# Two transformer blocks in float32 on one core: the boundaries between layers are reordered

## The chip, the cores and the metric

The kernel runs on one core of one Trainium2 chip. A core has TensorE (PE, matmuls into the eight banks of PSUM), VectorE (DVE), ScalarE (ACT), GpSimd (POOL, hardly used here) and SyncE (SP), whose queue issues all the DMAs of this kernel. Each engine runs its own instructions in order and waits on semaphores for the others. The metric is the device time of one launch in microseconds (us).

## The reference, cut to what is computed

Batch 1, 256 rows, width 2048, everything float32. The first block is a transformer block with a modulation from a vector c; the second has attention with compressed, selected and windowed keys, a pooling branch, cross attention to a memory, and a second feed-forward layer.

```python
ada = silu(c) @ w_ada + b_ada                 # shift, scale, gate for mixer and FFN
h = rms_norm(x, g_pre_mix) * (1 + scale_m) + shift_m
z = h @ w_in ; o = concat(mla(z), gla(z)) @ w_out
x = x + gate_m * rms_norm(o, g_post_mix)
h = rms_norm(x, g_pre_ffn) * (1 + scale_f) + shift_f
x = x + gate_f * rms_norm((silu(h @ w_ffn_gate) * (h @ w_ffn_up)) @ w_ffn_down, g_post_ffn)
# second block
z = rms_norm(x, ln_mix_pre) @ w_in_2          # 2048 x 7728
y = (g_a * (nsa(z) @ w_br_attn) + g_p * (pool(z) @ w_br_pool)) @ w_mix_out
x = x + rms_norm(y, ln_mix_post)
x = x + rms_norm(cross(rms_norm(x, ln_x_pre) @ w_xq, mem) @ w_xo, ln_x_post)
h = rms_norm(x, ln_ffn_pre)
x = x + rms_norm((silu(h @ w_gate) * (h @ w_up)) @ w_down, ln_ffn_post)
```

## The kernel before

**Tiling.** The 256 rows are two row blocks r = 0, 1 of 128 partitions (`RB`), and the width is 16 tiles of 128 (`KT`). The running sum is `X`. A product needs its left operand transposed: a *turn* takes 8 groups of two width tiles. For a group b PE transposes four 128x128 pieces into one bank (L1016), ACT rounds it to `XTh`, and DVE writes the rest, value less rounded value, to `XTl`. Turns used banks 4 and 5 in alternation (`PB[4 + g % 2]`), so PE could be two groups ahead of DVE (`turn_free`).

**Slabs.** Weights come in slabs of 1 MB (four width tiles by 512 columns, 454 in the first half of `w_in_2`), in a ring of four buffers `raw`. ACT rounds a slab to `wh` (`hi()`, L555), DVE writes the rest to `wl` (`lo()`, L1633), both with two buffers, and PE runs 24 matmuls (`slab_mm`, L1045 to L1047: four tiles, three products, first row block 0, then row block 1). `hi()` of a slab waits until the slab two before it is used up (`slab_used`). SP issues a new slab when DVE has finished with its buffer. Four slabs make a chunk of 512 columns, and a chunk has two banks, one for each row block.

**A layer's end.** The last product of a layer (`wout`, the FFN's `down`, `mix`, `xo`) leaves `ROWB`; ACT (L624) or DVE copies or adds a chunk, ACT squares it with a row sum (`post_square`, L548), DVE weighs it with the gain `G` (`weigh`, L1633). In `add_normed` DVE sums the squares (L1746), ACT takes the root, DVE inverts it (L1678), and eight instructions add the chunks to `X` (L1754); `x_added` counts them.

**A layer's start.** Five turns with their products follow: `f1` (first FFN), `z2` (`w_in_2`), `xq`, `f2`, and `o`, `y` without a norm. For `z2`, `xq` and `f2` the norm is taken after the product: PE turns `X` itself as soon as its chunks are added. For `f1` the norm comes first: ACT squares X in two instructions of 2048 columns (`norm_stats`), DVE inverts, ACT scales row block 0 and DVE row block 1 into `ROWB`, then PE turns `ROWB`; DVE applies scale and shift (`gained`, L1691) before ACT rounds. `turn_into` (L1020) turns four groups, runs slab 0, turns two groups, runs slab 1, and so on; `z2` alone turned all eight groups first (L1369).

**The order** is written out by hand, one stream for each engine. Chunk counts and semaphores are plain numbers.

```python
L1372                for c in range(2):
L1373                    chunk(c, ALL, Z2_PARTS[0][1], free=...)
```

## Time and profile before

| | us |
|---|---|
| median of 3 runs | 2922.84 |
| lowest, highest | 2920.22, 2924.76 |
| the profiled execution | 2926.01 |
| its span, first to last instruction | 2924.2 |
| PE busy (mean granted clock) | 2685.9 (0.954 of full) |
| DVE, ACT busy | 1663.4, 1157.8 |

A timeline row gives start, duration, engine, line and form; xN is a merged run of N instructions, and the brackets name the idle time just before and what ended it. PE's matmuls are pipelined: a row's 0.39 us is longer than its distance from the next.

### The profile page before, as it was taken

How to read it: one execution, taken by the hardware profiler on the slowest of the kernel's cores; microseconds unless marked ns; L12 is line 12 of the kernel's file. 1: busy time of each engine (PE TensorE's matmuls, PEld its weight loads, DVE VectorE, ACT ScalarE, POOL GpSimd, SP SyncE). 2: the span in 40 equal slices, each digit the busy share in tenths (PEclk: the TensorE clock that was granted, in tenths of full speed). 3: DMA queues.
4: the chain of work that ended last, by engine and by line, in shares of the span. 5: the costliest groups of instructions: out<-in, count | busy, mean ns of one | idle time of the engine just before them, and what ended most of it. 6: DMA issues, size and time to landing. Idle time of an engine off the chain costs nothing.

```text
span 2924.2 us, 31137 instructions
## 1 busy us (share of the span) xinstructions
PE 2685.9 (92%) x12176; PEld 2194.6 (75%) x12176; DVE 1663.4 (57%) x1601; ACT 1157.8 (40%) x1200; POOL 0.2 (0%) x4
## 2 busy tenths in 40 slices
...
DMA packets 253356, 565.93 MB, mean 194 GB/s; under 512 B 9647, under 2 KB 52557, under 8 KB 240094
## 3 DMA queue, kind: packets, MB, share of 16 engines
...
## 4 chain that ended last, share of the span: by engine, by line
PE 78%; DVE 8%; ACT 5%; DMA 4%; issue 4%; SPq 1%; DVEq 0%; ACTq 0%
PE bank L1045 23%; PE bank L1047 23%; PE bank L1046 23%; ACT wh L555 3%; DVE wl L1633 2%; DVE ACC L1654 2%; DMA raw<-in_w_ada 2%; DVE ROWB L1633 1%; DMA raw<-in_w_out 1%; DMA raw<-in_w_xkv 1%; PE bank L1016 1%; PE bank L1451 1%; DVE X L1754 1%; PE bank L1503 1%; PE bank L1082 1%
## 5 line engine op out<-in xcount | busy, mean ns | idle before, releaser
L1633 DVE TENSOR_TENSOR wl<-raw,wh 128x2048 fp32r<-128x2048 f32 (+2 forms) x430 | 975.3, 2269 | 912.2 <-ACT wh L555 911.5
L555 ACT ACTIVATE wh<-raw 128x2048 fp32r<-128x2048 f32 (+2 forms) x430 | 816.0, 1898 | 1260.6 <-PE bank L1047 1158.8
L1045 PE MATMUL bank<-wh,XTh 128*128 128x512 f32 (+2 forms) x2712 | 1077.6, 397 | 46.3 <-DVE wl L1633 36.7
L1046 PE MATMUL bank<-wl,XTh 128*128 128x512 f32 (+2 forms) x2712 | 1064.1, 392 | 0.0
L1047 PE MATMUL bank<-wh,XTl 128*128 128x512 f32 (+2 forms) x2712 | 1063.5, 392 | 0.0
L1045 PEld LDWEIGHTS bank<-wh,XTh 128*128 128x128 f32 x2712 | 520.4, 192 | 158.4 <-DVE wl L1633 31.5
L1047 PEld LDWEIGHTS bank<-wh,XTl 128*128 128x128 f32 x2712 | 518.9, 191 | 103.4
L1046 PEld LDWEIGHTS bank<-wl,XTh 128*128 128x128 f32 x2712 | 520.9, 192 | 99.0
L1045 PE MATMUL bank<-wh,HTh 128*128 128x512 f32 x704 | 276.7, 393 | 9.4 <-DVE HTl L1633 3.6
L1047 PE MATMUL bank<-wh,HTl 128*128 128x512 f32 x704 | 274.2, 389 | 0.0
L1046 PE MATMUL bank<-wl,HTh 128*128 128x512 f32 x704 | 274.1, 389 | 0.0
L1045 PEld LDWEIGHTS bank<-wh,HTh 128*128 128x128 f32 x704 | 132.1, 188 | 46.5 <-issue 14.4
L1047 PEld LDWEIGHTS bank<-wh,HTl 128*128 128x128 f32 x704 | 132.2, 188 | 27.7
L1046 PEld LDWEIGHTS bank<-wl,HTh 128*128 128x128 f32 x704 | 132.2, 188 | 26.6
L1654 DVE SCALAR_TENSOR_TENSOR ACC<-raw,cT,ACC 128x2048 f32<-128x2048 f32 x60 | 141.0, 2350 | 7.2 <-DMA raw<-in_w_ada 2.2
L1633 DVE TENSOR_TENSOR ROWB<-ROWB,bank 128x512 f32<-128x512 f32 x176 | 112.6, 681 | 10.9 <-PE bank L1047 9.0
L1650 DVE SCALAR_TENSOR_TENSOR ACC<-raw,cT,ACC 128x2048 f32<-128x2048 f32 x32 | 75.2, 2351 | 4.2 <-DVE wl L1633 1.6
L1016 PE MATMUL bank<-CON,ROWB 128*128 128x128 f32 x96 | 19.1, 355 | 48.2 <-ACT ROWB L548 17.1
L821 ACT ACTIVATE HTh<-bank 128x512 fp32r<-128x512 f32 x44 | 23.9, 595 | 90.4 <-PE bank L1331 90.4
L1016 PEld LDWEIGHTS bank<-CON,ROWB 128*128 128x128 f32 x96 | 14.2, 180 | 53.3 <-ACT ROWB L548 18.0
L548 ACT ACTIVATE XTh<-bank,vT 128x256 fp32r<-128x256 f32 x70 | 28.8, 471 | 47.7 <-PE bank L1016 47.6
L1016 PE MATMUL bank<-CON,X 128*128 128x128 f32 x96 | 19.8, 375 | 27.3 <-DVE X L1754 17.2
...
## 6 DMA issues: line engine op xcount, KB each, us to landing
...
```

Source lines behind the costliest of these rows:

```text
L555: act.activation(wh[:, st.lin % 2, 0:width], raw[:, st.raw % 4, 0:width], ACT.Copy).then_inc(hi_made, 1)
L1016: mm = pe.transpose(PB[4 + g % 2][:, SEQ * k + P * r:SEQ * k + P * r + P], src(r, 2 * b + k), ident)
L1045: pe.matmul(out_, hi_t[:, k, rows], w[0][:, q, :], start=first and q == 0, stop=False)
L1046: pe.matmul(out_, hi_t[:, k, rows], w[1][:, q, :], start=False, stop=False)
L1047: mm = pe.matmul(out_, lo_t[:, k, rows], w[0][:, q, :], start=False, stop=last and q == n - 1)
L1082: mm = pe.matmul(PB[7][:, k:k + 1], ACC[:, P * k:P * k + P], ones[:, 0:1], start=True, stop=True)
L1451: pe.matmul(PB[2 + u % 2][:, 0:2 * nk].rearrange("p (b n) -> p b n", b=2), QT(i, par, r), KT2(g, nk), start=True, stop=True).then_inc(S("n ...
L1503: pe.matmul(PB[7][:, HD * b:HD * b + HD], pT[:, u % 2, P * blk_:P * blk_ + P], Z2[:, k, c0:c0 + HD], start=k == 0, stop=k == r)
L1633: return dve.tensor_tensor(out_, a, b, op)
L1650: ins = dve.scalar_tensor_tensor(ACC[:, :], w, cT[:, bass.ds(k0 + k, 1)], ACC[:, :], ALU.mult, ALU.add)
L1654: ins = dve.scalar_tensor_tensor(ACC[:, :], w, cT[:, k:k + 1], ACC[:, :], ALU.mult, ALU.add)
L1754: dve.scalar_tensor_tensor(x, y, nstat[:, j, 2, r:r + 1], x, ALU.mult, ALU.add).then_inc(S("x_added"), 1)
```

## The change

- **First row block signalled alone.** The last slab of `wout`, `mix`, `xo` and of both `down` products increments a semaphore (`o_row`, `mix_row`, `xo_row`, `y_row`) after its first 12 matmuls. ACT copies and squares row block 0 then, and row block 1 after `slab_used`; DVE's last `add` does the same. ACT's order becomes copy, square, copy, square.
- **Root table early.** A one-column `Sqrt` into a new tile `warm` stands before the last chunk's copies and squares, so that the table load stands there and no longer behind them.
- **Residual squares per chunk.** For `f1` ACT squares `X` in eight pieces of 512, each when that piece has been added (`fsq`); DVE sums them. Both row blocks are then scaled in pieces of 512, and PE waits for a piece (`f_rows0`, `f_rows1`), not for the row. `mod_fin(4)` moves behind `add_normed("o")`.
- **Turns over four banks.** `f1`, `z2`, `f2`, `y`, `xq`, `o` use banks 4 to 7.
- **Projection begun on two groups.** `z2` is turned as the others are, by `turn_into`, with three `hi()` and three `lo()` in the turn; its loop of 2 x 2 chunks is written out as four chunks, and ACT's norm statistics come after the third `hi()`.

```diff
+WIDE = {"f1", "z2", "f2", "y", "xq", "o"}
+def turn_bank(name, b):
+    return 4 + (b % 4 if name in WIDE else (TURN0[name] + b) % 2)
...
+            def root_ready():
+                act.activation(warm[:, :], eps[:, 0:1], ACT.Sqrt)
+
+            def added_stats(name, ready):
+                j = NORMS.index(name)
+                for c in range(4):
+                    for r in range(RB):
+                        act.wait_ge(S("x_added"), added(ready, c, r + 1))
+                        if 2 * c + r >= 4:
+                            act.wait_ge(S("f_sq"), 2 * c + r - 3)
+                        k = 512 * ((2 * c + r) % 4)
+                        f(JUNK[:, k:k + 512], X[:, r, 512 * c:512 * c + 512], ACT.Square, "f_sq", accum_out=fsq[:, r, c:c + 1])
+                act.wait_ge(S("squared"), RB * j + RB)
+                f(nstat[:, j, 1, :], nstat[:, j, 0, :], ACT.Sqrt, "rooted", scale=1.0 / D, bias=eps[:, 0:1])
...
             def chunk_squared(name, layer, c, done):
+                if c == 3:
+                    root_ready()
+                    n = CHUNK0[layer] + c
+                    for r in range(RB):
+                        act.wait_ge(S(f"{name}_row"), 1) if r == 0 else act.wait_ge(slab_used, done)
+                        act.activation(ROWB[:, r, 512 * c:512 * c + 512], PB[2 * (n % 2) + r][:, :], ACT.Copy).then_inc(chunk_out, 1)
+                        post_square(name, c, lambda r: act.wait_ge(chunk_out, RB * n + r + 1), (r,))
+                    return
...
                 if k == 0:
-                    norm_stats(pre, lambda r: X[:, r, :], D, after)
-                    norm_rows(pre, lambda r: X[:, r, :], lambda r: ROWB[:, r, :])
+                    added_stats(pre, after)
+                    act.wait_ge(S("rooted_inv"), NORMS.index(pre) + 1)
+                    for c in range(4):
+                        f(ROWB[:, 0, 512 * c:512 * c + 512], X[:, 0, 512 * c:512 * c + 512], ACT.Copy, "f_rows0",
+                          scale=nstat[:, NORMS.index(pre), 2, 0:1])
...
-            turn_hi("z2", XTh, gain=vT[:, V_LN_MIX:V_LN_MIX + KT])
+            turn_hi("z2", XTh, gain=vT[:, V_LN_MIX:V_LN_MIX + KT], between=lambda: hi(4 * width))
             norm_stats("z2", lambda r: X[:, r, :], D, "y1")
...
                     g = TURN0[name] + b
-                    if g >= 2:
+                    if name in WIDE:
+                        pe.wait_ge(S("turn_free"), TURN0[name] + max(0, b - 3))
+                    elif g >= 2:
                         pe.wait_ge(S("turn_free"), g - 1)
                     if after:
                         pe.wait_ge(S("x_added"), added(after, b // 2))
+                    if each:
+                        each(b)
...
                     if half and r == 0:
-                        mm.then_inc(S("first_row"), 1)
+                        mm.then_inc(S(half), 1)
...
-            turn("z2", lambda r, k: X[:, r, P * k:P * k + P], lambda: None, after="y1")
-            turned_ready("z2")
-            with pe.Fori(0, 2) as i, st.loop(i, 2, 8, 8):
-                for c in range(2):
-                    chunk(c, ALL, Z2_PARTS[0][1], free=i * 4 + RB * (CHUNK0["zin2"] + c - 1))
+            for c in range(4):
+                chunk(c, ALL, Z2_PARTS[0][1], free=RB * (CHUNK0["zin2"] + c - 1), turning=None if c else (
+                    "z2", lambda r, k: X[:, r, P * k:P * k + P], lambda: None, "y1"))
...
-            mod_fin(4)
             add_normed("o")
+            mod_fin(4)
...
                 if k == 0:
-                    norm_row2(pre)
+                    j = NORMS.index(pre)
+                    dve.wait_ge(S("f_sq"), 4 * RB)
+                    dve.tensor_reduce(nstat[:, j, 0, :], fsq[:, :, :], AX.X, ALU.add).then_inc(S("squared"), RB)
+                    norm_inv(pre)
+                    dve.wait_ge(S("rooted_inv"), j + 1)
+                    for c in range(4):
+                        dve.tensor_scalar(ROWB[:, 1, 512 * c:512 * c + 512], X[:, 1, 512 * c:512 * c + 512],
+                                          nstat[:, j, 2, 1:2], None, ALU.mult).then_inc(S("f_rows1"), 1)
...
-                    add(n, FN - 1, last)
+                    add(n, FN - 1, last, k + 1 if n == 3 else None)
```

ACT between the last product of `w_out` and the turn `f1`, before (psq holds the layer's squares, nstat the norms' sums and roots):

```order
L624 ACTIVATE ROWB<-bank 128x512 x2
L548 ACTIVATE JUNK,psq<-ROWB 128x512 x2
L548 ACT_TABLE_LOAD
L548 ACTIVATE nstat<-nstat,eps 128x2
L548 ACTIVATE JUNK,nstat<-X 128x2048 x2
L548 ACTIVATE nstat<-nstat,eps 128x2
L548 ACTIVATE ROWB<-X,nstat 128x2048
L548 ACTIVATE XTh<-TMP 128x512 x4
```

The same place after the change:

```order
L599 ACT_TABLE_LOAD
L599 ACTIVATE warm<-eps 128x1
L806 ACTIVATE ROWB<-bank 128x512
L556 ACTIVATE JUNK,psq<-ROWB 128x512
L806 ACTIVATE ROWB<-bank 128x512
L556 ACTIVATE JUNK,psq<-ROWB 128x512
L556 ACTIVATE nstat<-nstat,eps 128x2
L556 ACTIVATE JUNK,fsq<-X 128x512 x8
L556 ACTIVATE nstat<-nstat,eps 128x2
L556 ACTIVATE ROWB<-X,nstat 128x512 x4
L556 ACTIVATE XTh<-TMP 128x512 x4
```

The table load stands ahead of the copies, each copy is followed by its square, and the two squares of `X` have become eight.

DVE at the same place, before:

```order
L1633 TENSOR_TENSOR mtmp<-bank,bT 128x16
L1668 SCALAR_TENSOR_TENSOR modA<-mtmp,vT 128x16
L1746 TENSOR_REDUCE nstat<-psq 128x2
L1633 TENSOR_TENSOR ROWB<-ROWB,G 128x512 x2
L1678 RECIPROCAL nstat<-nstat 128x2
L1754 SCALAR_TENSOR_TENSOR X<-ROWB,nstat,X 128x512 x8
L1678 RECIPROCAL nstat<-nstat 128x2
L1732 TENSOR_SCALAR ROWB<-X,nstat 128x2048
L1691 TENSOR_SCALAR TMP<-bank,modA 128x256 x4
L1633 TENSOR_TENSOR XTl<-TMP,XTh 128x512
```

And after:

```order
L1793 TENSOR_REDUCE nstat<-psq 128x2
L1678 TENSOR_TENSOR ROWB<-ROWB,G 128x512 x2
L1723 RECIPROCAL nstat<-nstat 128x2
L1801 SCALAR_TENSOR_TENSOR X<-ROWB,nstat,X 128x512 x8
L1678 TENSOR_TENSOR mtmp<-bank,bT 128x16
L1713 SCALAR_TENSOR_TENSOR modA<-mtmp,vT 128x16
L2012 TENSOR_REDUCE nstat<-fsq 128x2
L1723 RECIPROCAL nstat<-nstat 128x2
L2016 TENSOR_SCALAR ROWB<-X,nstat 128x512 x4
L1738 TENSOR_SCALAR TMP<-bank,modA 128x256 x4
L1678 TENSOR_TENSOR XTl<-TMP,XTh 128x512
```

The two small instructions on `mtmp` and `modA` now stand behind the eight additions to `X`, and a second sum of squares, of `fsq`, has come in.

ACT between the last squares of the first FFN and the first copy-out of `w_in_2`, before (the first rows only of its loop):

```order
L548 ACT_TABLE_LOAD
L548 ACTIVATE nstat<-nstat,eps 128x2
L548 ACTIVATE XTh<-bank,vT 128x256 x16
L548 ACTIVATE JUNK,nstat<-X 128x2048 x2
L548 ACTIVATE nstat<-nstat,eps 128x2
L555 ACTIVATE wh<-raw 128x1816
L857 UNCONDITIONAL_BRANCH
L857 ISA
L554 ISA
L555 ACTIVATE wh<-raw 128x1816
```

And after:

```order
L556 ACTIVATE JUNK,psq<-ROWB 128x512 x2
L556 ACTIVATE nstat<-nstat,eps 128x2
L556 ACTIVATE XTh<-bank,vT 128x256 x8
L563 ACTIVATE wh<-raw 128x1816
L556 ACTIVATE XTh<-bank,vT 128x256 x4
L563 ACTIVATE wh<-raw 128x1816
L556 ACTIVATE XTh<-bank,vT 128x256 x4
L563 ACTIVATE wh<-raw 128x1816
L556 ACTIVATE JUNK,nstat<-X 128x2048 x2
L556 ACTIVATE nstat<-nstat,eps 128x2
L563 ACTIVATE wh<-raw 128x1816 x2
L899 ACTIVATE Z_78<-bank,nstat 128x454 x2
```

The 16 roundings of the turn `z2` are broken into 8, 4 and 4 with one slab's `hi()` behind each, and the norm's squares have moved behind the third of them. On PE the 32 transposes that stood in one row become 16, 8 and 8 with the 24 matmuls of a slab between.

## Rows read from the trace of the kernel before

**Rows 1.** Timeline (start, duration), ACT: end of `wout` to turn `f1`.

```profile
605.26 1.08 ACT L624 ACTIVATE ROWB<-bank 128x512 f32<-128x512 f32 x2 [2.83 <-PE bank L1047]
...
619.98 2.00 ACT L548 ACTIVATE ROWB<-X,nstat 128x2048 f32<-128x2048 f32 x1 [0.30 <-DVE nstat L1678]
```

**Rows 2.** Timeline, DVE: the same place.

```profile
608.73 0.17 DVE L1633 TENSOR_TENSOR mtmp<-bank,bT 128x16 f32<-128x16 f32 x1 [3.67 <-PE bank L1082]
...
609.10 1.28 DVE L1633 TENSOR_TENSOR ROWB<-ROWB,G 128x512 f32<-128x512 f32 x2
...
610.50 5.39 DVE L1754 SCALAR_TENSOR_TENSOR X<-ROWB,nstat,X 128x512 f32<-128x512 f32 x8
...
623.21 1.90 DVE L1691 TENSOR_SCALAR TMP<-bank,modA 128x256 f32<-128x256 f32 x4 [1.94 <-PE bank L1016]
625.03 0.68 DVE L1633 TENSOR_TENSOR XTl<-TMP,XTh 128x512 fp32r<-128x512 f32 x1
```

**Rows 3.** Timeline, PE: turn `f1`, slabs 0 and 1.

```profile
622.09 1.94 PE L1016 MATMUL bank<-CON,ROWB 128*128 128x128 f32 x8 [13.40 <-issue]
...
629.34 0.78 PE L1045 MATMUL bank<-wh,XTh 128*128 128x512 f32 x1
...
636.70 0.60 PE L1016 MATMUL bank<-CON,ROWB 128*128 128x128 f32 x4
...
641.28 0.76 PE L1045 MATMUL bank<-wh,XTh 128*128 128x512 f32 x1 [1.63 <-DVE wl L1633]
```

**Rows 4.** Timeline, DVE, then PE: first FFN's end, turn `z2`, its slab 0.

```profile
1397.15 2.29 DVE L1633 TENSOR_TENSOR wl<-raw,wh 128x2048 fp32r<-128x2048 f32 x1 [1.41 <-ACT wh L555]
...
1408.56 1.66 DVE L1708 SCALAR_TENSOR_TENSOR XTl<-bank,vT,XTh 128x256 fp32r<-128x256 f32 x4
...
1419.49 0.74 PE L1045 MATMUL bank<-wh,XTh 128*128 128x454 f32 x1 [2.12 <-DVE XTl L1708]
```

**Rows 5.** Timeline, ACT: norm squares, `hi()` of slabs 2 and 5 of `z2`.

```profile
1418.14 1.91 ACT L548 ACTIVATE JUNK<-X 128x2048 f32<-128x2048 f32 x1
...
1427.31 1.72 ACT L555 ACTIVATE wh<-raw 128x1816 fp32r<-128x1816 f32 x1 [2.79 <-PE bank L1047]
...
1442.14 1.73 ACT L555 ACTIVATE wh<-raw 128x1816 fp32r<-128x1816 f32 x1 [3.22 <-PE bank L1047]
```

**Rows 6.** Timeline, DVE, then PE: end of `mix`, turn `xq`.

```profile
2075.78 0.16 DVE L1746 TENSOR_REDUCE nstat<-psq 128x2 f32<-128x8 f32 x1 [3.54 <-ACT JUNK L548]
...
2077.52 5.39 DVE L1754 SCALAR_TENSOR_TENSOR X<-ROWB,nstat,X 128x512 f32<-128x512 f32 x8
...
2085.38 0.78 PE L1045 MATMUL bank<-wh,XTh 128*128 128x512 f32 x1
```

**Rows 7.** Timeline, ACT: end of `xo`.

```profile
2149.92 0.63 ACT L548 ACTIVATE JUNK<-ROWB 128x512 f32<-128x512 f32 x1
...
2151.91 1.08 ACT L624 ACTIVATE ROWB<-bank 128x512 f32<-128x512 f32 x2 [1.27 <-PE bank L1047]
...
2154.23 1.28 ACT L548 ACT_TABLE_LOAD   x1
2155.53 0.29 ACT L548 ACTIVATE nstat<-nstat,eps 128x2 f32<-128x2 f32 x1
```

**Rows 8.** Timeline, PE: third and fourth groups of turns `o` and `y`.

```profile
508.90 1.25 PE L1016 MATMUL bank<-CON,Z 128*128 128x128 f32 x8 [1.78 <-DVE XTl L1633]
...
1982.02 1.97 PE L1016 MATMUL bank<-CON,Z 128*128 128x128 f32 x8 [0.56 <-DVE XTl L1633]
```

**Rows 9.** Timeline, DVE: the last `add`, at the kernel's end.

```profile
2911.58 1.29 DVE L1633 TENSOR_TENSOR ROWB<-ROWB,bank 128x512 f32<-128x512 f32 x2 [3.43 <-PE bank L1047]
```

**Rows 10.** Windows: length, busy of PE, PEld, DVE, ACT, POOL; granted clock; DMA share, GB/s.

```profile
1423.00:1426.00 3.00, 3.00 (x11) 2.65 (x11) 1.46 (x1) 1.51 (x1) 0.00 (x0) 0.65 0.00 0
2086.00:2089.00 3.00, 3.00 (x12) 2.41 (x11) 2.07 (x5) 2.40 (x3) 0.00 (x0) 0.78 0.99 384
644.00:648.00 4.00, 4.00 (x13) 3.18 (x12) 0.00 (x0) 0.51 (x1) 0.00 (x0) 0.64 0.41 159
```

More of the change, by code:

```diff
@@ L242, in build @@
         psq = sb("psq", [P, len(POST), RB, 4])
+        fsq = sb("fsq", [P, RB, 4])
+        warm = sb("warm", [P, 1])
         eps = sb("eps", [P, 1])
@@ L1003, in _, with turn @@
             st = Slabs()
-            def turn(name, src, ready, groups=None, after=None):
+            def turn(name, src, ready, groups=None, after=None, each=None):
                 ready()
@@ L1026, in turn_into, with slab_mm @@
                     if s < 2:
-                        turn(name, src, lambda: None, range(4 + 2 * s, 6 + 2 * s), after)
+                        turn(name, src, lambda: None, range(4 + 2 * s, 6 + 2 * s), after, each)
             def turned_ready(name):
                 pe.wait_ge(S("turn_free"), TURN0[name] + TURN_N[name])
-            def slab_mm(banks, kts, width, first, last, lhs=None, half=False, row_free=None):
+            def slab_mm(banks, kts, width, first, last, lhs=None, half=None, row_free=None):
                 hi_t, lo_t = lhs or (XTh, XTl)
@@ L1579, in _ @@
             for c in range(4):
-                chunk(CHUNK0["mix"] + c, ALL, 512, turning=None if c else (
+                chunk(CHUNK0["mix"] + c, ALL, 512, row="mix_row" if c == 3 else None, turning=None if c else (
                     "y", lambda r, k: Z2[:, r, P * k:P * k + P], lambda: pe.wait_ge(S("merged"), 3 * RB * 4)))
@@ L1622, in _ @@
             for c in range(4):
-                chunk(CHUNK0["xo"] + c, [12, 13, 14, 15], 512)
+                chunk(CHUNK0["xo"] + c, [12, 13, 14, 15], 512, row="xo_row" if c == 3 else None)
             ffn(1, "f2")
@@ L2001, in add @@
                     for r in range(RB):
+                        if row is not None and r:
+                            dve.wait_ge(slab_used, used)
                         y = ROWB[:, r, 512 * n:512 * n + 512]
```

75 lines of the change are left out of this document (41 added, 34 removed).

## The prediction

> **What bounds the kernel now.** I read the busy table first: PE works 2685.9 us of a span of 2924.2, DVE 1663.4 and ACT 1157.8. Then the timeline around each layer boundary, one engine at a time, to see which engine's last row releases the next. Inside a layer PE runs slab behind slab and the others wait for it, so nothing saved there on ACT or DVE counts. At a boundary the reverse holds: PE has nothing until the sum `X` is complete and turned. After `wout`, DVE's additions begin at 610.50 and take 5.39 [rows 2], the next transposes start at 622.09 after 13.40 us without a matmul, and slab 0 starts at 629.34 [rows 3]. The change touches only such stretches. What counts is therefore how much closer the first slabs of a layer come to the last matmul of the layer before. All sums are differences within the profiled execution (2926.01, span 2924.2); I subtract them from the median 2922.84, since the profiled one lies 0.1% above it and the stretches are fixed lengths.
>
> **wout to f1: 8.0 us, in three terms.**
> First the tail. Before, ACT starts its two copies at 605.26 [rows 1] and DVE's additions start at 610.50. The sum of squares is held back by `mod_fin`, which DVE does ahead of it and which waits for PE until 608.73; the weighing then takes 1.28 [rows 2]. After, the first row block is signalled half a slab (about 2.7) earlier, near 602.5, inside ACT's idle 2.83 [rows 1]. The table load (1.28) [rows 7] stands there too, so row block 0 is copied and squared (0.54 + 0.63) by 605.3. Row block 1 follows at 605.26: copy, then square with its accumulator read, done by 606.7. DVE reduces at 606.75, and from a reduction to the additions it needs 0.15 + 1.28 + 0.16, here 1.5 with overlaps: additions from 608.27, a gain of 2.2. `mod_fin` now runs behind the additions. Its two instructions of 0.17 [rows 2] end at 614.0, while ACT still squares (below): cost nothing; uncovered it would be 0.35.
> Second the norm. Before, the additions end at 615.89 and the transposes start at 622.09 [rows 2, 3]: 6.2, of which two squares of 2048 columns (1.91 each, row of the same form in [rows 5]) and the scaling of row block 0, 2.00 [rows 1]. After, ACT squares each piece of 512 in 0.63 [rows 7], below the addition's pace of 5.39/8 = 0.67, so it ends one piece behind: additions end at 613.66, squares at 614.42, reduction 0.15, root 0.29, reciprocal 0.17. Scaling starts at 615.25 and PE after its first piece at 615.95, i.e. 2.3 behind the additions instead of 6.2: gain 3.9. ACT's later pieces (0.63 each) stay ahead of PE, which needs 0.97 for a group. DVE's pieces have no row; bounds are 0.4 (row of 256 columns, 1.90/4 less 0.07) and 0.68 [rows 2], and with either they keep pace too.
> Third the turn. Before, with two banks, transposes to slab 0 took 7.25 (622.09 to 629.34) [rows 3]. After, four groups lie in four banks at once, and DVE sets the pace: one group transposed (about 1.1), four `gained` groups less the last (3 x 0.95) and two rests (0.68 each, overlapping a little), 5.4. Gain 1.85. Slab 0 takes until 636.70 and slab 1 starts 4.6 later [rows 3], because DVE does two groups and `lo()` between; that order is unchanged, so this gap stays.
> Sum 2.2 + 3.9 + 1.85 = 8.0.
>
> **y1 and z2: 7.0 us.** At the end of the first FFN the early signal helps nothing: DVE runs its last `lo()` from 1397.15 to 1399.44 [rows 4] and goes from there into the final add, the sum and the additions without a pause. Tail 0. Call T = 1408.56 the end of the additions. Before, eight groups are turned, then slab 0 starts at 1419.49 (T + 10.9) [rows 4]. Slab 2 is being rounded from 1427.31 and slab 5 from 1442.14, each released by the end of the slab two before [rows 5]; so slab 0 ends at 1427.3, slab 3 ends and slab 4 starts at 1442.1 (T + 33.5), and the pitch is 14.83/3 = 4.94 per slab. After, PE has four groups in four banks as the chunks are added, DVE finishes groups 0 and 1 with four rests (1.66) [rows 4] and slab 0 starts at T + 1.7. Slab 0 some 6.4, transposes 1.0, slab 1 4.94: T + 14.1. But the norm is later now: behind slab 1 ACT and DVE still have roundings of the last groups (1.6), a `hi()` (1.72), two squares (3.9), root and reciprocal (0.6), another `hi()` (1.72) and a `lo()` (2.05, the row of 2.29 scaled to 454 columns), 12.1 in all, where PE has slabs 2 and 3 to work on (9.9 and two transposes 1.0). PE runs dry by about 1.2 and slab 4 starts at T + 26.4: 7.0 earlier. The bounds: the 9.2 gained at slab 0 is kept but for the two groups of transposes that now lie behind it (8.5), or the three `hi()` and `lo()` in the turn each hold a slab by 1.5 (4.0). The loop becoming straight code adds no row I can see; its branch instructions lie on idle sequencers.
>
> **The four-bank turns of xq, f2, o and y: 2.7 us.** At `xq` the additions end at 2077.52 + 5.39 = 2082.91 and slab 0 starts at 2085.38 [rows 6], 2.47 later; with groups 2 and 3 already transposed only the four rests of 1.66 remain: 0.8. `f2` is built alike: 0.8. At `o` and `y` PE waited 1.78 and 0.56 for a bank [rows 8]; that wait goes, but `o` is fed by weights that arrive slowly, so I take 0.6 and 0.5. Bounds 0 and 2.3 for the two together.
>
> **Tails of mix, xo and y2: 1.27 - 0.25 + 0.64.** At `mix` the sum of squares comes at 2075.78 [rows 6], after two copies and two squares; with row block 0 done earlier one copy (0.5) and square are left out: 2074.78. The table load (1.28 between squares and root, as in [rows 7]) held the root; without it the additions follow 1.47 behind (0.15 + 1.28 + 0.16 less overlap, as at `wout`): 2076.25 against 2077.52. At `xo` ACT is not idle: it squares chunk 2 until 2150.6 and copies again from 2151.91, with an idle of 1.27 [rows 7]. Load and `warm` (1.5) overrun that idle, and four serial instructions follow; I find the additions at 2156.3 against 2156.06, a loss of 0.25. Bounds: gain 1.3 as at `mix`, loss 1.6. At the kernel's end the two adds take 1.29 together [rows 9]; one of them moves ahead: 0.64.
> The trace has the root 0.02 behind the load's end (2154.23 + 1.28 to 2155.53) [rows 7]. The Trainium skill (ScalarE: Activation LUTs, "What ACT_TABLE_LOAD costs") puts a drain of 1380 ns on top of the load; no pause of that kind stands in this row, and with it `xo` would lose about 1.6 and the total would be 1.4 us smaller. I go by the row.
>
> **Sum.** 8.0 + 7.0 + 2.7 + 1.27 - 0.25 + 0.64 = 19.4. 2922.84 - 19.4 = **2903.5**. SP's queue loses and gains no DMA; a buffer is reissued when DVE's `lo()` is done, which only comes earlier. PE's new waits (`turn_free`, `x_added`, `f_rows`) hold transposes alone, and behind them only the slab that needs them.
>
> **The clock** is the term I can't sum. In windows right after slab 0's start the granted clock is 0.65 at `z2`, 0.78 at `xq`, 0.64 within slab 1 of `f1` [rows 10]: part at 1.2 and part at 2.4 GHz. Slab 0 took 7.4 at `f1` (629.34 to 636.70), 7.8 at `z2` (1419.49 to 1427.31), against 4.94. Where the transposes ran straight into the slab (`xq`) the clock was back sooner than where PE had waited in between. After the change PE transposes four groups in one go, then pauses about 1.4. I take the two as balancing.
>
> **Rivals.**
> A. *The turn warms the clock.* Four groups without a pause count as work, and slab 0 runs at the full clock at `f1`, `z2`, `xq`, `f2`: about 1.8 each (the 2.4 to 2.9 that the rows show at `f1` and `z2`, the 1.1 of `xq`, averaged), 7.2 in all: 2896.3. For: `xq`'s early return. Against: the pause that follows. 0.12.
> B. *The clock comes later.* The new pause, and fewer transposes close to slab 0, leave slab 0 slow at `xq` and `f2` (1.0 each) and slab 1 partly slow at `z2`, `xq`, `f2` as it is at `f1` (2.9 each): 10.7 lost, 2914.2. For: [rows 10] at `f1`. 0.13. Beside it stands the Trainium skill (TensorE: Matmul & The Clock Gate, "Part 4: PE-mode transpose"): transposes don't count as PE-busy in the same way. This trace speaks partly against that, as `xq` shows.
> C. *The waits were covered by something else* (weights at the boundaries arrive no sooner, or the stretch gained is given back at the first slab that waits for DMA): 2922, no change. Against: the ring of four slabs is full through each tail. 0.04.
> D. *Slower.* The turns now split PE's start into short bursts with pauses, and the clock stays at 1.2 GHz through the first slabs. A slab at that level costs another 4.9 (twice the pitch). Four such slabs beyond those of today eat the 19.4, from there it is slower; with 14 (three more at most boundaries) 2922.8 - 19.4 + 69 = 2972. Against: before, slabs behind pauses of 13 us still regained the clock within one or two. 0.03.
> The forecast itself: 0.68, with a range of its own of 2898 to 2909 (`z2` 4 to 8.5, the turns, `xo`).
>
> **Numbers.** 0.2% is 5.8 us, about what a measurement here can tell from no change. Forecast, A and B are all faster by more: 0.93; same 0.04; slower 0.03. The range reaches into A and B: 2895 to 2914.5.
>
> **What the profile after would show.** Additions at `wout` start 3.0 behind ACT's last copy instead of 5.2; the first transposes of `f1` 2.3 behind their end, slab 0 5.4 later, slab 1 still 4.6 behind slab 0's end. At `z2` slab 0 at T + 1.7 and slab 4 at T + 26.4 with a small DVE wait before it. Additions at `mix` 2.9 behind the last matmul's release, at `xo` no earlier. Table loads ahead of the last copies. The forecast is wrong if slab 0 comes on time but the granted clock of the first two slabs differs from today's, if scaling of `ROWB` on DVE falls behind PE, or if `z2`'s norm holds slab 4 by more than 1.2.

## The result, and the profile after

The median of 4 runs is 2905.89 us (2903.01 to 2909.67) against 2923.11 for the kernel before; the ratio is 0.9943, 95% interval 0.9931 to 0.9955: 17 us less, with the interval reaching from 13 to 20. The forecast was 2903.5, its range 2895 to 2914.5. The profiled execution took 2907.55 us, its span is 2905.8, 18.4 shorter than the span before.

The page of the changed kernel, first its busy row, then its chain:

```profile
PE 2678.1 (92%) x12176; PEld 2189.3 (75%) x12176; DVE 1662.8 (57%) x1605; ACT 1160.4 (40%) x1220; POOL 0.2 (0%) x4
...
PE 77%; DVE 9%; ACT 5%; DMA 5%; issue 3%; SPq 1%; DVEq 0%; ACTq 0%
```

PE's work is the same, so what went away is time between its slabs. To say where, I line up the starts of all slabs in the two timelines of PE. "Pause" below is the time from the start of a slab's last matmul to the start of the next slab's first one (0.23 in a gapless row of slabs), "length" that from a slab's first matmul to its 24th (5.21 at full clock for 512 columns, 4.74 for 454). Slab 62 is slab 0 of `f1` in this count, 194 that of `z2`, 276 of `y`, 292 of `xq`, 296 of `xo`, 300 of `f2`.

End of `wout` to `f1` in the changed kernel, timeline of ACT, DVE and PE (start, duration; to be held against [rows 1 to 3]):

```profile
601.19 1.92 ACT L563 ACTIVATE wh<-raw 128x2048 fp32r<-128x2048 f32 x1 [4.29 <-DMA raw<-in_w_ffn_gate]
603.12 1.28 ACT L599 ACT_TABLE_LOAD   x1
604.42 0.20 ACT L599 ACTIVATE warm<-eps 128x1 f32<-128x1 f32 x1
604.52 0.58 ACT L806 ACTIVATE ROWB<-bank 128x512 f32<-128x512 f32 x1
...
605.77 0.58 ACT L806 ACTIVATE ROWB<-bank 128x512 f32<-128x512 f32 x1
```

```profile
607.21 0.16 DVE L1793 TENSOR_REDUCE nstat<-psq 128x2 f32<-128x8 f32 x1 [1.78 <-ACT JUNK L556]
...
608.68 5.39 DVE L1801 SCALAR_TENSOR_TENSOR X<-ROWB,nstat,X 128x512 f32<-128x512 f32 x8
613.99 0.17 DVE L1678 TENSOR_TENSOR mtmp<-bank,bT 128x16 f32<-128x16 f32 x1
...
614.97 0.16 DVE L2012 TENSOR_REDUCE nstat<-fsq 128x2 f32<-128x8 f32 x1 [0.60 <-ACT JUNK L556]
...
615.69 1.67 DVE L2016 TENSOR_SCALAR ROWB<-X,nstat 128x512 f32<-128x512 f32 x4
```

```profile
616.67 3.65 PE L1056 MATMUL bank<-CON,ROWB 128*128 128x128 f32 x16 [7.92 <-DVE ROWB L2016]
622.05 0.79 PE L1085 MATMUL bank<-wh,XTh 128*128 128x512 f32 x1 [1.74 <-DVE XTl L1678]
...
633.94 0.76 PE L1085 MATMUL bank<-wh,XTh 128*128 128x512 f32 x1 [3.55 <-DVE wl L1678]
```

The additions start at 608.68 instead of 610.50, the transposes 2.6 behind their end instead of 6.2, and slab 0 5.4 behind the first transposes instead of 7.25. Slab 1 still starts 4.8 behind slab 0's last matmul.

`z2`, timeline of DVE and of PE (against [rows 4]):

```profile
1392.10 5.39 DVE L1801 SCALAR_TENSOR_TENSOR X<-ROWB,nstat,X 128x512 f32<-128x512 f32 x8
1397.41 3.22 DVE L1755 SCALAR_TENSOR_TENSOR XTl<-bank,vT,XTh 128x256 fp32r<-128x256 f32 x8
```

```profile
1399.11 0.47 PE L1085 MATMUL bank<-wh,XTh 128*128 128x454 f32 x1 [1.81 <-DVE XTl L1755]
...
1423.89 0.44 PE L1085 MATMUL bank<-wh,XTh 128*128 128x454 f32 x1 [1.09 <-DVE wl L1678]
```

With T = 1397.49, the end of the additions, slab 0 starts at T + 1.6 and slab 4 at T + 26.4, after the small wait of 1.1 for `lo()`, behind the norm's squares.

By place, in us gained, from the two profiles. The last two rows hold what no term of the forecast named. All cells together, with `o` at 0, make 18.6, and the span is 18.4 shorter; 2.8 of that (+2.6, -1.1, +1.3) stands at places that the experiments below show to be chance:

| place | forecast | measured | clock beside it |
|---|---|---|---|
| `o` turn | 0.6 | 0.4 in the pause before slab 0, 0 by the end of `wout` | |
| `wout` to `f1` slab 0 | 8.0 | 7.3 | 0 |
| `y1`, `z2` to slab 4 | 7.0 | 6.9, 1.0 of it clock in slab 0 | |
| wait for weights, slab 210 | 0 | -1.4 | -1.4 |
| `y` turn | 0.5 | 0.77 | -0.5 |
| `mix` tail, `xq` turn | 1.27 + 0.8 | 1.21 + 0.85 | -0.7 |
| `xo` tail, `f2` turn | -0.25 + 0.8 | -0.5 + 0.83 | +1.6 (slab 296), +0.9 (slab 300) |
| end | 0.64 | 0.6 | |
| slabs 70, 304, products before slab 118 | 0 | | +2.6, -1.1, +1.3 |
| slab 211 to the end of the second block's attention | 0 | -0.7 | |

### The profile page after: what moved, and what is told of

Read it like the earlier page. It is cut to its first block, busy times and chain, and to the rows that moved or that the text cites. A ratio compares the mean times of both kernels' runs of the same rounds, so it can differ in the third digit from the quotient of the medians.

```text
span 2905.8 us, 31119 instructions
## 1 busy us (share of the span) xinstructions
PE 2678.1 (92%) x12176; PEld 2189.3 (75%) x12176; DVE 1662.8 (57%) x1605; ACT 1160.4 (40%) x1220; POOL 0.2 (0%) x4
## 4 chain that ended last, share of the span: by engine, by line
PE 77%; DVE 9%; ACT 5%; DMA 5%; issue 3%; SPq 1%; DVEq 0%; ACTq 0%
PE bank L1085 23%; PE bank L1087 23%; PE bank L1086 23%; ACT wh L563 3%; DVE wl L1678 2%; DMA raw<-in_w_ada 2%; DVE ACC L1699 2%; DVE ROWB L1678 2%; DMA raw<-in_w_out 1%; DMA raw<-in_w_xkv 1%; PE bank L1496 1%; DVE X L1801 1%; PE bank L1056 1%; PE bank L1548 1%; ACT JUNK L556 1%
## 5 line engine op out<-in xcount | busy, mean ns | idle before, releaser
L1755 DVE SCALAR_TENSOR_TENSOR XTl<-bank,vT,XTh 128x256 fp32r<-128x256 f32 x70 | 29.0, 477 | 24.3 <-ACT XTh L556 24.3
```

## Experiments

Twelve kernels ran in three groups, two of them (the kernel before again, and the one with the loops of `z2`) for their trace only, one run each; the kernel before ran beside each group (medians 2923.04, 2927.31, 2924.06), and ratios are against that.

**The changed kernel and the kernel before, again.** No edit.

> The changed kernel, unaltered, a second time. Theory 1: where the granted clock falls and returns is not fixed by the program, so single slabs differ between two profiles of the same kernel. The slab behind the 3.97 us pause in the first FFN (start 684.59 in the first profile, 5.34 us long there, 8.21 in the kernel before) takes either about 5.3 or about 8.2, the starts of slabs elsewhere shift by the same amounts, and the sum of such differences is 1 to 4 us. Waits that the order of instructions sets (17.2 us before slab 0 of f1, 11.5 before slab 0 of z2, 1.45 before slab 4 of z2) repeat within 0.1. Theory 2: the clock's places are fixed by the program: every slab repeats within 0.1. Time 2903 to 2910 either way. The wait of 3.28 us for a weight slab after the loads of w1 and REL (1.88 in the kernel before): repeats within 0.3 if the change made it, between 1.5 and 3.5 if it is the DMA's own scatter.

Measured: 2904.01 us, ratio 0.9937 (0.9915 to 0.9959). Windows over six slabs that stand behind a pause (slabs 70, 194, 292, 296, 300, 304), one row each: length, busy times, granted clock, DMA share, GB/s. First before, then the changed kernel, then the changed kernel again:

```profile
691.90:700.10 8.20, 8.16 (x23) 6.47 (x24) 5.24 (x4) 1.42 (x1) 0.00 (x0) 0.62 0.52 158
...
2128.20:2135.20 7.00, 7.00 (x24) 5.64 (x25) 2.29 (x1) 0.91 (x1) 0.00 (x0) 0.76 0.36 112
...
2191.90:2199.00 7.10, 7.10 (x24) 5.67 (x25) 2.11 (x1) 1.59 (x3) 0.00 (x0) 0.76 0.85 290
```

```profile
684.60:692.80 8.20, 8.09 (x34) 6.40 (x35) 5.68 (x5) 3.29 (x2) 0.00 (x0) 1.00 0.51 158
...
2112.10:2119.10 7.00, 7.00 (x31) 5.78 (x32) 2.29 (x1) 2.06 (x2) 0.00 (x0) 1.00 0.36 109
...
2173.00:2180.10 7.10, 7.10 (x19) 5.62 (x20) 2.10 (x1) 1.58 (x3) 0.00 (x0) 0.59 0.84 292
```

```profile
679.50:687.70 8.20, 8.18 (x23) 6.51 (x24) 5.22 (x4) 1.39 (x1) 0.00 (x0) 0.62 0.52 161
...
2110.60:2117.60 7.00, 6.97 (x31) 5.75 (x32) 2.29 (x1) 2.06 (x2) 0.00 (x0) 1.00 0.37 104
...
2171.50:2178.60 7.10, 7.07 (x31) 5.87 (x32) 2.17 (x1) 2.89 (x4) 0.00 (x0) 1.00 0.81 286
```

Slab 70 ran at 0.62 before, at 1.00 in the first profile of the changed kernel and at 0.62 in the second: the 2.6 us that the first comparison credits there are chance, and so are the 1.1 at slab 304 and the 1.3 before slab 118 (a pause of 13.06 or 11.7 in profiles of either kernel). Slab 296 is not: 0.76 before, 1.00 in both. The pauses set by the order repeat within 0.05 at `z2` (11.49 and 11.50), `xq` (10.37, 10.36) and `f2` (12.09 twice), but at `f1` the pause is 17.17 and 17.96 us: in the second profile the gate weights landed later, ACT's `hi()` ended at 599.6 and the table load ran behind it, until both copies were late.

> The kernel before, unaltered, a second time, for its trace. Theory: what the order of instructions sets repeats within 0.1 us (24.5 us before slab 0 of f1, 20.75 before slab 0 of z2, 12.4 before xq and f2); slabs behind a pause change between about 5.3 and about 8.2 from profile to profile. Open: the wait for a weight slab behind the loads of w1, 1.88 here and 3.28, 3.28, 3.25, 3.27 and 3.13 in the five profiles of the changed kernel and its variants, and the first slab of xo, 6.97 here and 5.35 to 5.37 in the other five. If both repeat, the change moved them (a transfer and a clock that stand in another place to the pauses before them); if the wait comes out near 3.2 or the slab near 5.4, it was chance.

Measured: 2921.41 us in one run. Slab 70: 5.35 long here, 8.21 in the first profile. Slab 296: 6.93, against 6.97. Slabs 292 and 300: 6.29 both, against 6.22. The wait behind the loads of `w1`: 1.66, against 1.88. So the clock has two kinds of places. At slab 70 and slab 304, and in slabs 0 to 2 of `f1`, it differs from profile to profile (slab 70: 5.35, 6.95 and 8.2 all occur among the fourteen profiles). At `xq` and `xo` it goes with the program: `xo`'s first slab is 6.93 to 6.97 in both profiles of before and 5.34 to 5.39 in all twelve others; `xq`'s is 6.2 to 6.3 and 6.86 to 7.00. Which part of the change moved them stays open, since no run that takes one part back restores them. `y` and `f2` lie between: `y`'s first slab is 5.9 to 6.0 before and 6.04 to 6.43 after, and `f2`'s, 6.2 to 6.3 before, is 5.35 to 5.39 in six profiles that leave `f2`'s turn and tail as they are in the change, but 8.17 in a seventh (the run with `f1`'s norm whole).

**z2 turned at once.**

```diff
-turn_hi("z2", ..., between=lambda: hi(4 * width))
+turn_hi("z2", ...)                       # one hi() ahead of the four chunks, DVE likewise
-chunk(c, ..., turning=None if c else ("z2", ...))
+turn("z2", ..., after="y1"); turned_ready("z2"); chunk(c, ...)
```

> The changed kernel with one part undone: z2 turns all eight groups before its slab 0, as before, the norm's squares directly behind, but still over four banks. My sum puts 6.9 us of gain on this part, measured from the end of the additions to slab 4: then 2905.9 + 6.9 = 2912.8 less what four banks give here on their own (1 to 2 us, groups 2 and 3 need not wait for DVE): about 2911.5. Rival: the longer wait for weights after the loads of w1 (3.28 against 1.88, and 1.4 of clock behind it) was brought by the z2 part: it vanishes here and the kernel costs only 4 us more, about 2909. Rival: no loss at all, since the weights that come with the loads of w1 set the end of this stretch anyway: 2906.

Measured: 2905.17 us, ratio 0.9935 (0.9913 to 0.9957): no loss that this can tell. I compare the time from the start of the last slab of the first FFN to slab 4 of `z2`: before 48.54, changed 41.62, here 43.28. Slab 0 starts 4.7 later, but then nothing waits, and 1.7 remain. The expectation (2911.5, some 5.6 us more) was wrong: I had given the whole 6.9 to the early start. The wait for weights was 3.25 here too, so this part did not bring it.

**Two banks.**

```diff
-WIDE = {"f1", "z2", "f2", "y", "xq", "o"}
+WIDE = set()
```

> The changed kernel with the turns back on two banks, all else kept. Theory: f1's slab 0 starts 1.85 us later behind its first transposes (5.4 to 7.25), xq and f2 0.3 to 0.8 each, y 0.5 to 0.8, z2 about 1.1, o about 0.6 or hidden: 5 to 6 us more, about 2911. Rival: the clock gains nothing from four groups in one go, and PE's shorter pause before slab 0 keeps it up: slabs 0 of xq (6.96) and y (6.38) go back to 6.2 and 5.9, so that the loss is 1.2 smaller, about 2910. Rival: the four banks are worth nothing, 2906.

Measured: 2909.83 us, ratio 0.9959 (0.9945 to 0.9972), 10 runs. PE in the turn `f1`:

```profile
616.40 1.94 PE L1056 MATMUL bank<-CON,ROWB 128*128 128x128 f32 x8 [8.77 <-DVE ROWB L2016]
620.08 1.12 PE L1056 MATMUL bank<-CON,ROWB 128*128 128x128 f32 x4 [1.74 <-DVE XTl L1678]
622.89 1.11 PE L1056 MATMUL bank<-CON,ROWB 128*128 128x128 f32 x4 [1.69 <-DVE XTl L1678]
```

The two waits for DVE are back, slab 0 starts at 623.65, 7.25 behind 616.40. Pauses against the changed kernel: `y` 8.58 (7.81), `xq` 11.20 (10.36), `f2` 12.92 (12.09). With f1's 1.87 that is 4.3. The ratio is 0.0016 above the one in the section on the result and 0.0022 above the one of the changed kernel's second turn in the same group, 4.7 and 6.4 us. At `z2` the pause is 0.85 longer, but slab 0 takes 5.33 instead of 6.41, and the stretch to slab 4 is 41.36. The rival on the clock was half right: `xq`'s slab 0 stays at 6.89, `y`'s goes back to 6.04. And `f2`'s slab 0, which the rival did not name, takes 7.07 here against 5.39, so part of the loss in this profile is clock.

**z2 wholly as before.** Both edits above, the banks for `z2` alone.

> The changed kernel with z2 wholly as before: all eight groups at once and over two banks. Either half alone cost little when it was undone (all at once: slab 4 1.9 us later behind the additions; two banks at all turns: slab 0 of z2 0.9 later but 1.1 shorter). Theory: the two halves stand in for each other, as DVE's wait for a bank and the wait for all groups both lie between the additions and slab 0, and only together do they restore 20.75 us of idle time before slab 0 and the 6.9 us of my sum: slab 4 at T + 33.3, 2905.9 + 6.9 = 2912.8. Rival: the halves add, 1.9 + 0.9 = 2.8, 2908.7.

Measured: 2912.17 us, ratio 0.9950 (0.9934 to 0.9967). PE in the turn:

```profile
1396.34 1.97 PE L1057 MATMUL bank<-CON,X 128*128 128x128 f32 x8 [0.99 <-DVE XTl L1757]
1399.30 1.97 PE L1057 MATMUL bank<-CON,X 128*128 128x128 f32 x8 [0.99 <-DVE XTl L1757]
1403.11 0.75 PE L1086 MATMUL bank<-wh,XTh 128*128 128x454 f32 x1 [1.84 <-DVE XTl L1757]
```

The stretch to slab 4 is 48.16, 6.5 more than in the changed kernel, while the one half undone costs 1.7 and the other nothing. They stand in for each other, as the theory had it: either one alone brings most of the 7 us. It is the places in the trace that show this; the whole times, 0.9950 against 0.9943 and 0.9937, are 2 to 4 us apart with intervals that overlap. Slab 0 takes 6.41 here as in the changed kernel, not the 7.41 of before, so the 1.0 of clock that the table gives at `z2` doesn't come from the order of the turn. It went with the chunks written out: in the run with the loops of `z2` back slab 0 takes 7.48.

**Without first-row signal and early table.** The branch `if c == 3` of `chunk_squared`, `root_ready` and the `row` of `add` are taken out.

> The changed kernel without the signal of the first row block and without the early root table: copies and squares of the last chunk as in the kernel before, the table load back between squares and root. Theory, by place against the changed kernel: additions at w_out 0.7 us later, at mix 1.2 later (3.35 to 4.56 behind the last matmul), at xo 0.5 earlier (5.08 to 4.57), at the end 0.6 later, y1 nothing: in all 2.0 more, about 2907. Rival: the whole part is worth nothing at w_out because the norm behind it waits for ACT anyway: 1.3 more.

Measured: 2906.63 us, ratio 0.9927 (0.9910 to 0.9943). That is no loss against 0.9937 and 0.9943; 2 us are below what these intervals can tell, and the places in the trace carry the verdict. Pause before `xq` 11.58 instead of 10.36, 1.2 as expected; before `f2` 11.67 instead of 12.09, 0.4 less; before `f1` 17.94, at the upper end of what kernels that leave this place as the change has it show (16.7 to 18.0). So this part is worth 1.2 at `mix`. At `wout` it is worth between 0 and 1.2, by when the gate weights land: additions start 4.59 behind the last matmul here, 3.36 to 4.65 with the part, 5.67 in the kernel before; the 1.1 from 5.67 to 4.59 came without this part, with `mod_fin` moved behind the additions. At `xo` it costs 0.4 or nothing: additions start 4.66 behind the last matmul here and 4.57 in the kernel before, while the part in place gives 5.08 in six profiles but 4.72 and 4.73 in the runs with `f1`'s norm whole and with `z2`'s loops back, whose code at this place is the same. The difference is a hand-over: DVE's sum starts 0.46 behind ACT's last read of the accumulator in the changed kernel and 0.11 in the run with the loops.

**f1's norm whole.**

```diff
-added_stats(pre, after)                  # and rows in pieces of 512 on ACT and DVE
+norm_stats(pre, lambda r: X[:, r, :], D, after)
+norm_rows(pre, lambda r: X[:, r, :], lambda r: ROWB[:, r, :])
```

> The changed kernel with the norm of f1 as before: two squares of 2048 columns behind the additions, and rows scaled whole. Theory: additions' end to first transposes goes from 2.6 back to 6.2, slab 0 of f1 3.6 us later, about 2908.5. Rival: with a longer pause ahead of it the clock is lower at slab 0 and slab 1 too: another 1 to 2 us. Rival: 3.6 us are not lost, since the turn behind is set by DVE: 2905.

Measured: 2915.1 us, ratio 0.9950 (0.9932 to 0.9968). The additions end at 614.11 and PE's row reads:

```profile
620.31 3.64 PE L1053 MATMUL bank<-CON,ROWB 128*128 128x128 f32 x16 [10.09 <-issue]
```

6.2 us, as before; in the changed kernel 2.6. The 3.6 are as expected and go through to slab 0. Of the clock rival nothing can be said: slabs 0 to 2 took 8.26, 6.90 and 7.80, and they scatter as much in the changed kernel (7.08 and 5.33, 7.91 and 8.05, 6.76 and 6.82 in its two profiles).

**The loops of z2 back.**

```diff
-for c in range(4):                       # on PE, ACT and DVE
-    chunk(c, ALL, Z2_PARTS[0][1], free=RB * (CHUNK0["zin2"] + c - 1))
+with pe.Fori(0, 2) as i, st.loop(i, 2, 8, 8):
+    for c in range(2):
+        chunk(c, ALL, Z2_PARTS[0][1], free=i * 4 + RB * (CHUNK0["zin2"] + c - 1))
```

> The changed kernel with z2 wholly as before (eight groups at once, two banks) and also its 2 x 2 chunks back in loops on PE, ACT and DVE. For one question: the wait for the first weight slab behind the loads of w1 and REL was 1.88 and 1.66 in two profiles of the kernel before, and 3.13 to 3.57 in all eight of the changed kernel and its variants, z2 turned as before included. In that stretch the kernel before shows no transfer on the instruction queue, all eight others show one of 16 KB, and REL lands after 12.5 to 12.8 there, 13.9 to 14.3 here. Theory: the chunks written out made the program longer, so that a code load falls between those transfers; with loops it moves away and the wait is 1.9 or less, the slab behind it 4.8 instead of 6.1 to 7.5. Rival: it is the time at which the loads meet the weight slabs, not the code: the wait stays at 3.2 (or a code load falls there still, which the instruction queue will show).

Measured: 2907.47 us in one run. DMA queues in the 30 us in which `w1` and REL land, changed kernel and then this one (packets, MB, share; then per transfer the KB and the us to landing):

```profile
q1 hardware_dynamic: 8777, 8.10, 97.1%
q8 instruction: 1, 0.02, 0.2%
...
REL<-rel_scratch SPq DMA_DIRECT2D x1, 2048.0 KB, 14.0
```

```profile
q1 hardware_dynamic: 9061, 8.62, 101.9%
...
REL<-rel_scratch SPq DMA_DIRECT2D x1, 2048.0 KB, 12.8
```

Before the change the same stretch shows, as here, no transfer on the instruction queue. REL lands after 12.8 as in the kernel before. The wait for the next weight slab is 2.17, where the theory had 1.9 or less: 1.0 to 1.4 of the 3.1 to 3.6 have gone, 0.3 to 0.5 above before. The pages agree: 52 instruction packets before and here, 54 or 55 in all the others. So the theory holds for 1.0 to 1.4 us of the waiting: against the run with `z2` wholly as before, from which this one differs by the loops alone, 3.20 fell to 2.17, in one profile each. That it is the code load that delays REL is inferred from their always going together (three profiles without it: 12.5 to 12.8; eight with it: 13.9 to 14.3); no run moved the load alone. The slab behind it was expected at 4.8 and stayed slow, 6.37 against the 4.82 that stood behind a wait of 1.88 before.

**lo() first in the turn f1.** Not part of the change.

```diff
-for b in range(n + 1): gained(b); rest(b - 1); between() if b in (4, 6, 8)
+scale 0 1, rest 0, scale 2, rest 1, scale 3, rest 2 3, lo, scale 4 5, rest 4 5, lo, scale 6 7, rest 6 7, lo
```

> Not part of the change: in the turn f1, DVE makes lo() of the next slab before the scale and shift of groups 4 and 5, and 6 and 7 (order: scale 0 1, rest 0, scale 2, rest 1, scale 3, rest 2 3, lo, scale 4 5, rest 4 5, lo ...). PE now waits 4.81 us from the last matmul of slab 0 to slab 1 and again before slab 2; DVE is idle for 6.3 us during slab 0. Theory: both waits fall to about 1.0 as at xq, 7.6 us less, about 2898. Second step of the theory: the clock falls in those pauses (slab 1 takes 7.91 and slab 2 6.76, against 5.21), so with short pauses another 3 to 4 us come back: about 2894.5. Rival: the waits only move, since slab 2 needs groups 4 and 5, whose scale now stands behind lo(): slab 2 waits 3 us and the gain is 4: 2902.

Measured: 2890.76 us, ratio 0.9890 (0.9871 to 0.9910), 13 us below the changed kernel on the same chip. DVE, which in the changed kernel stood idle for 6.3 through slab 0:

```profile
622.80 2.29 DVE L1678 TENSOR_TENSOR wl<-raw,wh 128x2048 fp32r<-128x2048 f32 x1 [1.11 <-ACT wh L563]
628.33 1.90 DVE L1738 TENSOR_SCALAR TMP<-bank,modA 128x256 f32<-128x256 f32 x4 [3.24 <-PE bank L1056]
```

The pauses before slabs 1 and 2 are 1.02 and 1.36 instead of 4.81 twice, and the slabs take 5.33 and 5.32 instead of 7.9 and 6.8; new pauses of 1.30 and 1.07 stand before slabs 3 and 4: for slab 3 `lo()` waits for ACT's `hi()`, for slab 4 it stands behind eight memsets of `ROWB` on DVE (4.27). From slab 0 to slab 4 it is 28.9 us, against 37.0 and 35.5 in the two profiles of the changed kernel. Slab 0 itself ran at three different clocks in them (8.20, 7.08 and 5.33 long); from its last matmul to slab 4 it is 20.7 against 30.0 and 30.2, so the new order gives 9.3 of the 13, 5.3 of it in shorter pauses and 4 in slabs 1 and 2. The profile is of this kernel's longest run (2900.45; the other three are 2889 to 2892), with slab 70 at 8.26 and slab 304 at 8.11, so the rest may well be clock; the profile can't show it.

**Three changes more.** `lo()` first; the root table loaded before chunk 0 of each last layer; the nine small loads spread over `z2`:

```diff
+if c == 0: root_ready()                  # was c == 3
+for c, s: slab(w_in_2 ...); if 4 * c + s >= 6 and side: load(*side.pop(0))
```

> The changed kernel with three things of mine added: DVE's lo() ahead of the scale in the turn f1 (as in the run before), the root table loaded before the first chunk of each last layer and not before the fourth, and the nine small loads for the compression weights and REL each behind one weight slab of z2, from the seventh slab on, instead of all behind the sixteenth. Theory, against the changed kernel: f1 7.6 and 2 to 4 of clock; additions behind the last matmul at xo 3.15 instead of 5.08, at w_out 0.5 earlier, together 2.4; the wait of 3.28 and the slow slab behind it gone: 2.8 to 4.6. Sum 15 to 18: 1.2% below the kernel before plus 0.2: ratio 0.988 to 0.989 at the least, 0.9875 likely. Rival: the small loads only move their delay to slabs 7 to 15 of z2, where the ring of four is less full: nothing gained there, or a loss of up to 3.

Measured: 2890.9 us, ratio 0.9887 (0.9870 to 0.9903). It is as good as `lo()` first alone (0.9890) and not better by a measurable amount, though its profile shows both parts at work: the pause before slab 210 is 0.21 instead of 3.28, the slab 4.74 instead of 6.1; the pause before `f2` 10.72 instead of 12.09. The rival (the loads' delay only moves) is out, as no slab of `z2` waits. The places sum to 5.8 us, but `f2`'s slab 0 takes 6.96 here (6.92 and 6.97 in the two kernels below, which share this part) instead of 5.35 to 5.39, so the clock takes back all of the 1.4 that the earlier additions at `xo` gave. The other 4 us the median doesn't show; the intervals (±0.17%, 5 us) are wide enough to hide them.

**PE kept busy in the pauses.** 20 or 22 idle matmuls before the transposes and 4 behind them; then the same with 30 and 7 transposes.

```diff
+for i in range(n): pe.matmul(PB[q][:, 0:454], w[:, i % 4, 0:P], w[:, (i + 1) % 4, :], start=True, stop=True)
```

> The kernel with three more, and PE kept busy in its pauses at f1, z2, xq and f2: 20 to 22 matmuls of 454 columns on a finished weight slab (results overwritten by slab 0) before the first transposes, 4 between the transposes and slab 0. Nothing of the computation changes. It prices the clock. Theory: the slabs behind those pauses run at full clock: slab 0 5.3 instead of 6.4 to 8.2 at f1, z2 4.8 instead of 6.4, xq 5.3 instead of 7.0, f2 unchanged at 5.35: 5 to 7 us less than the kernel without them. Rival: the clock falls through other pauses all the same and the extra matmuls stand in the way of the transposes: no change or 1 to 2 us more.

> As the run with matmuls in the pauses, but with 30 and 7 transposes of 128 columns (float32, as the turns use) in their place, of about the same length. It tells whether transposes hold the clock. Theory 1: they do as well as matmuls, and slab 0 is as short as there. Theory 2: they don't count in the same way: slab 0 stays at 6.4 to 8.2 at f1, 6.4 at z2 and 7.0 at xq, and the time is that of the kernel without them.

Measured: 2892.42 and 2893.71 us, ratios 0.9887 (0.9871 to 0.9904) and 0.9891 (0.9875 to 0.9908), as without them; the 5 to 7 us of the theory did not come. Slab 0 of `z2` and of `xq`, windows of the kernel with neither, with matmuls, with transposes (granted clock third from the end):

```profile
1388.30:1394.80 6.50, 6.46 (x24) 5.78 (x25) 3.50 (x5) 0.71 (x1) 0.00 (x0) 0.74 0.27 67
2051.10:2058.10 7.00, 6.92 (x23) 5.59 (x24) 3.79 (x6) 0.83 (x1) 0.00 (x0) 0.76 0.96 363
```

```profile
1394.80:1399.70 4.90, 4.85 (x24) 4.45 (x25) 3.52 (x5) 0.00 (x0) 0.00 (x0) 1.00 0.07 10
2058.00:2065.00 7.00, 6.94 (x23) 5.57 (x24) 3.77 (x6) 0.09 (x1) 0.00 (x0) 0.76 0.98 360
```

```profile
1393.20:1398.10 4.90, 4.89 (x24) 4.49 (x25) 3.47 (x5) 0.00 (x0) 0.00 (x0) 1.00 0.10 10
2056.50:2063.50 7.00, 6.91 (x23) 5.55 (x24) 3.80 (x6) 0.13 (x1) 0.00 (x0) 0.76 0.96 363
```

At `z2` either filling brings slab 0 to the full 2.4 GHz: 4.84 long in both instead of 6.41, 1.6 us. The transposes of the turn behind the fillers run at that clock too, 8 in 1.06. At `xq` and `f2` neither does anything (6.97 and 6.96, 6.92 and 6.97; 6.96 at both without). At `f1` the test failed: the fillers stood behind PE's wait for `mod_fin`, which the change has put behind the additions:

```profile
613.56 7.13 PE L1064 MATMUL bank<-wh 128*128 128x454 f32 x22 [5.24 <-DVE modA L1741]
620.52 1.91 PE L1083 MATMUL bank<-CON,ROWB 128*128 128x128 f32 x16
```

They began as the rows were nearly ready and held the transposes up: slab 0 starts 4.2 later behind the additions with matmuls and 2.4 later with transposes, which ate what `z2` gained. In no place did transposes do other than matmuls. The Trainium skill (TensorE: Matmul & The Clock Gate, "Part 4: PE-mode transpose") says that transposes don't count as PE-busy in the same way; in this kernel, float32 and in these pauses, no difference shows. Only `z2` can tell, as nothing else answered to either filling, and the profile lists the transposes as plain MATMUL rows, so it doesn't show the mode they ran in.

## Why the prediction was right, and where it was not

The time came out 2.4 us above the forecast, inside the forecast's own range, and for the stated reasons at most places. One of its own signs of being wrong did appear: slab 0 came on time and its clock differed from before, at `z2` (6.41 long for 7.41), `xq` (6.97 for 6.23) and `f2` (5.35 for 6.22). Point by point:

- **wout to f1**, 8.0 forecast, 7.3 measured. Norm 3.9, measured 3.6 (the run with the whole norm gives the 3.6 back); turn 1.85, measured 1.87. The tail was over-sized, 2.2 against 1.9. The step that failed put the table load at 602.5, into ACT's idle 2.83 [rows 1]. That idle begins where `hi()` of an arriving gate slab ends, and the end moves with the DMA: 603.1 here, 599.6 against an earlier last matmul in the next profile. The first copy started at 604.52 where the forecast needs 604.1, the second at 605.77 for 605.26. Where the gate weights landed earlier against the last matmul, as in four of the variants (table load 2.1 to 3.0 ahead of it), the additions start 3.4 behind it instead of 5.67: the 2.2 of the forecast is there.
- **z2**, 7.0 forecast, 6.9 measured, with T + 1.7 / T + 26.4 against 1.6 / 26.4, and the stall of 1.1 before slab 4 where I had 1.2. The mechanism was right, the closeness is in part luck. The six items that make "12.1 in all" sum to 11.6, which would put slab 4 at T + 25.7. The items were well sized (11.5 from the first rounding at 1412.22), but that rounding started 0.6 behind slab 1's end, which no item held. And slab 0 at "some 6.4", against 7.4 before, had no row: 1.0 of clock stood inside this term while the clock was priced at nothing. The attribution was not separable: undoing the early start costs 1.7, undoing the banks nothing, undoing both 6.5. I had worked out only both together, which is all that the forecast needed, and then wrongly gave 5 to 7 to one of them when I set out the experiment.
- **Four-bank turns** 0.8, 0.8, 0.5: 0.85, 0.83, 0.77; at `o` the pause before slab 0 shrank by 0.4 (49.04 to 48.64; 49.03 with two banks), but `wout` waits for weights in between, and its last matmul starts at 604.88 for 604.83.
- **Tails.** `mix` 1.21 for 1.27, end 0.6 for 0.64. `xo` lost 0.5, not 0.25: from 4.57 to 5.08 behind the last matmul. Sign and cause were right (load and four serial instructions on a busy ACT). In the changed kernel's two profiles the size was short by 0.25; in two of its variants that share this place the additions start 4.7 behind, a loss of 0.15. Behind the load ACT goes on 0.02 later (the rows of the load at 603.12 and of `warm` at 604.42 show the same), so the drain of 1380 ns that the Trainium skill states (ScalarE: Activation LUTs, "What ACT_TABLE_LOAD costs") does not appear in this kernel.
- **"The loop becoming straight code adds no row I can see"** was the wrong sentence. It adds two code loads, one of which falls among REL's packets and goes with 1.0 to 1.4 of waiting; 1.4 of clock in the slab behind comes with the longer wait, though it did not leave with the code load. Nothing in the trace of before could have shown it there, but the instruction queue is listed on the page and I did not price it.
- **The clock** at zero net: the places that repeat in both profiles of each kernel give +1.0 (`z2`, already inside its 6.9), +1.6 (`xo`), +0.9 (`f2`), -0.5 (`y`), -0.7 (`xq`), -1.4 (slab 210), together +0.9, of which `f2`'s and `y`'s move in variants that leave them alone. The excess that rival A is built on was read too large at `f1`: its slab has 512 columns and takes 5.21 at full clock, not the 4.94 of `z2`'s pitch, so 1.9 and not 2.4. That the net came near zero is partly luck, since the parts are up to 1.6 and I named neither `xo` nor slab 210.

Of the rivals, A (full clock in slab 0 everywhere) is out: lengths are 7.1, 6.4, 7.0 and 5.35 against 5.2 or 4.7, and only `f2` did as it says. B was right in one half at one place (`xq` 0.7 slower) and out elsewhere, and no slab 1 of `z2`, `xq`, `f2` was slow (4.84, 5.33, 5.33). C and D are out.

## What to carry to other kernels

Where two edits remove waits that lie side by side before the same instruction, measure the pair and each alone: here one of them alone brings 5 to 7 of the 7 us. Look at the engine that stands idle while PE works through the first slab; the order of its queue (here `lo()` behind the scale of the next groups) was worth more than any single part of this change. Before a clock difference in one profile is credited to an edit, take a second profile of the same kernel: single slabs moved by 2.9 us between two of them.

## What the runs showed of the chip

- Behind the same pause of 3.97 us, slab 70 took 5.35, 6.95 or 8.2 us with this place of the kernel unchanged (5.35 and 8.2 in two profiles of the very same kernel, granted 1.00 and 0.62), while `xo`'s first slab, behind 18.2 us, took 6.93 to 6.97 in the two profiles of before and 5.34 to 5.39 in the twelve others.
- The low clock need not begin with the slab: at `xq` the first matmuls behind a pause of 10.4 us were 0.23 apart, as at 2.4 GHz, then seven were 0.43 apart, as at 1.2 GHz, and the rest 0.23 again.
- A 16 KB code load on the instruction queue went with 1.1 to 1.8 us more for a transfer of 2 MB in small packets (12.5 to 12.8 against 13.9 to 14.3).
- Filling a pause with float32 transposes (3.5 us, and 0.9 behind the turn) or with matmuls of rounded operands (4.3 and 1.1) had the same effect on the clock behind it, full at one place and none at two.
